# Hybrid decoder trunk on one core: places of the mixing steps in the other stage's program from two tables, in place of even spacing

## The reference, cut to what matters

```python
h = rms_norm(x, norm_mix_g[i]);  z = h @ w_cols
zs = token_shift(z[..., :RWKV_COLS], mu_shift[i])       # r, k, v and three low-rank inputs
...
y = rwkv7_scan(rh, decay, kh, vh, kk, a)                # 8 heads x 64, a state passed from token to token
swa_out = swa_sink_attention(zq, zk, zvv, sinks[i], rel_bias)   # window 128, 8 query heads, 2 kv heads
x = x + concatenate([rwkv_out, swa_out]) @ w_out[i]
u = rms_norm(x, norm_mlp_g[i])
x = x + square(relu(u @ w_ff_up[i])) @ w_ff_down[i]
e = rms_norm(p[i] @ ple_proj[i], ple_norm_g[i])
x = x + e * sigmoid(x @ ple_gate[i])
return rms_norm(x, final_norm_g)
```

## The kernel before

| step | TensorE | waits for |
|---|---|---|
| 0, 1 | keys and scores; decay and rate (L703) | step 1: `small` by ScalarE |
| 2, 3 | norms; transposed probabilities (L672) | step 3: probabilities (L1397) by VectorE's step 2, which waits for ScalarE's step 1 and goes on with the scan (L1423) and a scaling (L1427) |
| 4, 5, 6 | norms spread; output gate; bonus (L735) | `knorm`, `kk`, `rk` by VectorE |
| 7 to 9 | second half of the attention, transposes | probabilities again (L1397) |
| 10, 11 | scores of the recurrence (L766); `av` | `kappa_t`; masked scores |
| 12 to 16 | five doubling steps of the inverse (L787) | VectorE: add, mask, transpose (L1494) |
| 17 to 23 | the inverse put together; state (L828), both chunks | the step before, by VectorE |
| 24 | `y` | nothing new; behind it GpSimd squares `y` (L543) |
| 27 | `y` transposed (L876) | the normed `y` (L1544); behind it VectorE makes `rw` (L1549) and GpSimd adds and multiplies (L546, L549) |
| 28 | nothing | SyncE stores `rw` (L426) |

## Time and profile before

### The profile page before, as it was taken

How to read it: one execution, slowest core, us unless ns; L and a number is a source line. 1 busy time by engine, 2 the same in 40 slices (tenths; PEclk the granted TensorE clock), 3 DMA queues, 4 the chain that set the end, 5 groups by cost and what they waited for, 6 DMA issues and landing times.

```text
span 3061.8 us, 54864 instructions
## 1 busy us (share of the span) xinstructions
PE 2866.5 (94%) x23922; PEld 2282.5 (75%) x23922; DVE 1350.0 (44%) x2329; ACT 1187.6 (39%) x1939; POOL 1146.6 (37%) x540
## 2 busy tenths in 40 slices
PE   7988989999999989989999999998999899999997
PEld 6767767777777767767777777776777678788876
DVE  4265474535444344563535353644453535311114
ACT  4354344244434242453443333534242425422224
POOL 3433333342334333433333333324344334344442
PEclk9999999999999999999999999999999999999999
DMA  6532433353232313342223233332232224333332
GB/s 201 182 115 89 132 109 94 109 182 91 63 97 73 99 59 99 121 147 66 86 80 92 66 99 101 128 101 77 81 97 78 61 88 149 117 97 96 97 97 76
DMA packets 335948, 313.31 MB, mean 102 GB/s; under 512 B 13499, under 2 KB 288220, under 8 KB 335708
## 3 DMA queue, kind: packets, MB, share of 16 engines
q1 hardware_dynamic: 331312, 305.38, 32.5%
q10 hardware_dynamic: 4396, 4.41, 0.5%
HBM read 271.98 MB, written 39.32 MB: 102 GB/s over the span
## 4 chain that ended last, share of the span: by engine, by line
PE 64%; DVE 8%; ACT 5%; POOL 3%; issue 3%; ACTq 0%; POOLq 0%; DVEq 0%
PE ps L895 11%; PE ps L899 10%; PE ps L898 10%; PE ps L943 7%; PE ps L947 6%; PE ps L946 6%; POOL w_lo L505 2%; PE ps L641 1%; PE ps L787 1%; PE ps L644 1%; ACT bm L1108 1%; PE ps L645 1%; ACT work L1130 1%; PE ps L663 1%; PE ps L680 1%
## 5 line engine op out<-in xcount | busy, mean ns | idle before, releaser
L505 POOL TENSOR_TENSOR w_lo<-wraw_f,w_hi 128x1024 fp32r<-128x1024 f32 x408 | 990.9, 2429 | 1600.2 <-ACT w_hi L1025 1600.0
L1025 ACT ACTIVATE w_hi<-wraw_f 128x1024 fp32r<-128x1024 f32 x408 | 430.3, 1055 | 643.6 <-PE ps L895 550.2
L895 PE MATMUL ps<-w_hi,h_hi 128*128 128x512 f32 x1280 | 525.0, 410 | 26.2 <-POOL w_lo L505 19.7
L899 PE MATMUL ps<-w_hi,h_lo 128*128 128x512 f32 x1280 | 503.3, 393 | 0.0
L898 PE MATMUL ps<-w_lo,h_hi 128*128 128x512 f32 x1280 | 502.7, 393 | 0.0
L943 PE MATMUL ps<-act_hi,w_hi 128*128 128x512 f32 x1024 | 423.9, 414 | 27.0 <-DVE x L1604 19.6
L946 PE MATMUL ps<-act_lo,w_hi 128*128 128x512 f32 x1024 | 405.8, 396 | 0.0
L947 PE MATMUL ps<-act_hi,w_lo 128*128 128x512 f32 x1024 | 405.2, 396 | 0.0
L895 PEld LDWEIGHTS ps<-w_hi,h_hi 128*128 128x128 f32 x1280 | 242.4, 189 | 94.1 <-POOL w_lo L505 27.6
L1214 ACT ACTIVATE h_hi<-tmp 128x512 fp32r<-128x512 f32 x128 | 80.9, 632 | 545.9 <-DVE tmp L1586 545.9
L899 PEld LDWEIGHTS ps<-w_hi,h_lo 128*128 128x128 f32 x1280 | 242.3, 189 | 53.0
(11 more groups left out here) (223 smaller groups left out, 4428.6 us busy)
## 6 DMA issues: line engine op xcount, KB each, us to landing
wraw_f<-in_w_ff_up SPq DMA_DIRECT2D x256, 256.0 KB, 3.4
wraw_f<-in_w_ff_down SPq DMA_DIRECT2D x128, 512.0 KB, 3.8
wraw_f<-in_w_in SPq DMA_DIRECT2D x80, 512.0 KB, 4.4
zT<-tmp SPq DMA_DIRECT2D x80, 256.0 KB, 2.1
wraw_f<-in_w_out SPq DMA_DIRECT2D x32, 512.0 KB, 5.0
wraw_f<-in_w_gate SPq DMA_DIRECT2D x32, 512.0 KB, 3.9
zs<-zT SPq DMA_DIRECT2D x16, 896.0 KB, 7.4
h_lo<-mixT SPq DMA_DIRECT2D x4, 2048.0 KB, 9.8
```

Of the source, the lines that this page charges most:

```text
L505: G.tensor_tensor(w_lo[:, n % 2, :], raw[:, n % 4, :], w_hi[:, n % 2, :].bitcast(F32), ALU.subtract).then_inc(w_lo_done, 1)
L895: mm = T.matmul(ps[:, j, :], ah, wh, start=(first and k == 0), stop=False)
L899: mm = T.matmul(ps[:, j, :], al, wh, start=False, stop=(final and k == 1))
L1025: S.activation(w_hi[:, n % 2, :], raw[:, n % 4, :], ACT.Copy).then_inc(w_hi_done, 1)
```

## The change

`side_by_side` takes a tuple of 116 places instead of a number of quanta and a head. Before, step i stood at `head + (quanta - head) * i // 116`: from 4 to 113 beside the projection, from 2 to 148 beside a finish (gaps of 1 and 2 in a fixed rhythm). Now the places are read from two tables. All engines still run the same instructions; only the order in which steps and quanta follow each other in each engine's program differs, the same on all five.

```diff
-LEAD = 150
-def side_by_side(fill, tiles, quanta, head):
-    given, steps = 0, MIX_STEPS * len(tiles)
-    for i in range(steps):
-        want = head + (quanta - head) * i // steps
-        while given < want:
+BESIDE_PROJ = (3, 4, 4, 5, 7, 8, 10, 13, 14, 14, 14, 15, 17, 19, 21, 22, 24, 25, 26, 27, 27, 27, 27, 28, 28, 29, 29, 31, 31, 32, 34,
...
+BESIDE_FIN = (0, 1, 3, 4, 5, 5, 7, 7, 8, 9, 10, 13, 13, 14, 15, 19, 21, 23, 24, 26, 27, 29, 30, 31, 31, 33, 33, 35, 36, 36, 37, 39,
...
+def side_by_side(fill, tiles, places):
+    assert len(places) == MIX_STEPS * len(tiles)
+    given = 0
+    for i, place in enumerate(places):
+        while given < place:
             next(fill)
             given += 1
         next(tiles[i // MIX_STEPS])
...
-    side_by_side(one_after_another(proj(1), proj(2), proj(3)), [mix(t) for t in range(TPB)], 3 * 2 * ZT - 6, 4)
+    side_by_side(one_after_another(proj(1), proj(2), proj(3)), [mix(t) for t in range(TPB)], BESIDE_PROJ)
     for b in range(1, BLOCKS):
-        side_by_side(fin(b - 1), [mix(t) for t in range(b * TPB, (b + 1) * TPB)], LEAD, 2)
+        side_by_side(fin(b - 1), [mix(t) for t in range(b * TPB, (b + 1) * TPB)], BESIDE_FIN)
```

## The result

The changed kernel takes 2918.09 us (median of four runs, 2913.71 to 2920.3) against 3063.01 for the kernel before, measured beside it on the same chips (3059.04 to 3066.16). The ratio is 0.9526, with a 95% interval of 0.9508 to 0.9543 (the later intervals are of the same kind): 145 us faster. The forecast was 76 us, with a range that ended 12 us above what was measured. The direction was right, the size was half.

The account below looks back on a forecast made before the run. TensorE, busy 2866.5 of 3061.8 us, was taken as the bound. Three finish blocks at 28 us (21 waits, 5 clock, 2 turns) plus 18 in the projection made 102; a quarter off, 76, gave 2984 us, range 2930 to 3035.

Parts of the forecast that it names:

- rival 1: The forecast itself: a good part of TensorE's waits goes, 2930 to 3035 us; chance 0.79.
- Part (b): Steps with GpSimd work at a chunk's start delay the next chunk's `w_lo`: 1.2 to 3.1 us each; mid-chunk, no wait.
- The clock: Stretches at 1.2 GHz follow waits of over about 2 us; 5 us a finish block recoverable, 4 in the projection.
- Rival 3: Slower: 27 steps at gap 0 wait for their predecessor, up to 6.9 us each, 3110 us; chance 0.07.
- Rival 4: More goes, the clock recovering altogether and tiles not disturbing each other: below 2930 us; chance 0.04.
- the projection stage: Stage ahead of the finish blocks: 10 us of idle time, 4 of clock and 4 of turns saved, 18 us.
- the turns: TensorE turning to a step and back, 0.2 us estimated; fewer turns save 2 us a finish block, 4 in the projection.
- A quarter off gives 76 us: Discount on the 102 us sum for two conflicts in a row or a queue not seen.
- The residual waits, 17 us a block: TensorE idle time left in a finish block, against 38 us before: 21 us saved.
- Step 12 at gap 0: First doubling step of tiles 0, 1 and 3 beside a finish, no quantum ahead: 1.6 us each.
- Step 24 at 66: Tile 1's step ahead of which GpSimd squares `y`, at a chunk's start beside a finish: about 1.2 us lost.
- Steps 27 and 28 at 156: Tile 3 beside a finish: `rw` queued behind VectorE's transpose work, the second gate chunk behind `rw`, 3.5 us.

Follow-up runs that it names:

- e4: Even spacing (the kernel before) with steps 24, 27 and 28 beside each finish moved one quantum, off chunk starts: 3033.13 us (0.9904).
- e10: Changed kernel with a gap of 1 instead of 0 ahead of step 12 of tiles 0, 1 and 3 beside each finish: 2920.21 us (0.9529).
- e12: Changed kernel with step 27 of tile 3 at place 154 instead of 156 beside each finish: 2917.49 us (0.9522).
- e13: Changed kernel with only step 1 of each tile beside each finish one quantum later, at chunk starts (2, 38, 72, 112): 2943.14 us (0.9605).
- e14: Even spacing with the moves of e4, steps 0 to 3 and neighbours moved, step 1 in the middle of its chunk in all tiles: 2986.48 us (0.9745).
- e11: Even spacing with the moves of e4 and some twenty more, step 1 at a chunk's start in tiles 0, 2 and 3: 3016.25 us (0.9847).
- e8: Changed kernel with a smoothed table: projection places remade with fewer gaps of 0, some finish steps of tiles 0, 1 and 3 moved: 2938.58 us (0.9598).
- e9: Changed kernel with steps 27, 28 of tiles 1 and 2 at chunk starts, the next tile's steps 0 and 1 one quantum behind: 2945.69 us (0.9615).
- e5: Changed kernel with every place of the finish table one quantum higher, all gaps the same: 3050.85 us (0.996).
- e1: New finish table alone, old even spacing beside the projection: 2936.72 us (0.9589).
- e6: Changed kernel with every place of the finish table two quanta higher, all gaps the same: 2983.18 us (0.9739).

## Why the prediction was wrong

**Held.** What bounds the kernel, the repetition of three equal blocks and the untouched last one. The mechanism of rival 1: waits go, TensorE's work is the same. Part (b) for steps 24 and 27: its prices make 7.6 us a block, 23 in three, with the clock behind them on top, and e4 measured 30. Three entries of the residual list: step 5 at gap 0 (predicted 0.9, measured 0.95 from start to start), step 1 of tile 1 at 37 (2.0 and 1.8), the transposes ahead of the gate (2.3 and 2.2 from start to start). The clock: 5 us a block predicted, 6.2 measured (31 distances between fill matmuls of 0.43 us in place of 0.23 became none: 31 x 0.20). Rival 3, slower by gaps of 0, did not come: no wait at such a gap in the finish block is above 1 us, and in the projection stage they reach 2.1. Rival 4, below 2930, had 0.04 and is what happened.

**Right by luck: the projection stage.** 18 us were predicted and 18.2 measured, but of other parts. Idle time fell by 14.7 us where I had 10, the clock gave about 2.4 (12 fewer distances at half rate) where I had 4, and about 1 is left for the turns, where I had 4. Single terms were further off: the waits for the probabilities, of which I had 3.2 us of new ones in tile 0, fell from 6.0 to 0.8; the bonus fell to 0, not to 2; step 1 of tile 2, whose 3.1 us were to go with one quantum, still waits 2.26. The number itself is loose: nine traces with this projection table reach the first finish block between 643.0 and 649.7 us, six with even places between 661.9 and 669.7.

**Failed: the sum per finish block**, in two terms. The gap of 70 us between 76 and 145.6 is 26 from the first, and 43 from the second with the smaller terms beside it.

1. *"A quarter off gives 76 us."* I took a discount for conflicts that I had not seen. No such loss showed in the total: the sum of 102 was already low, not high. 26 us.
2. *The residual waits, 17 us a block.* Measured: 7.2 of idle time. Step 12 at gap 0, three times 1.6, cost 0 (e10; its operand hangs on step 10, not 11). Step 24 at 66, 1.2, cost 0. Steps 27 and 28 at 156, 3.5, cost 0.8, and moving step 27 to 154 doesn't get it (e12). The bonus, step 11, "a step behind adds" and the weight chunk, 2.2, cost 0. Together nearly 11 us of the 17 were not there, and about 1 us stood where I had none (the transposes at quanta 17 to 20). So 31 us of idle time went, where I had 21. About 4 us more a block are an estimate: there are 20 waits fewer, and each makes the matmul behind it some 0.2 us later than its idle time says (the one at 1451.13 waits 3.08 us and starts 3.47 behind the one before it, in place of 0.23). With 6.2 of clock that leaves about 3 for the turns in the block, whose length fell by 44.3; I had 28. The three blocks gave 127.5 for 84.

Two of the signs were wrong too: TensorE's busy time was to stay within 10 us and fell by 42, and the idle time ahead of the doubling steps was to stay or rise and fell from 6.6 to 0 us in the finish block, from 9.0 to 5.6 in the projection stage.

**Not seen: step 1's side of the chunk.** Part (b) of the prediction looked at GpSimd, since the profile names GpSimd's `w_lo` as the releaser. Part of these waits come from ScalarE, one engine further up: in the block of before, GpSimd had been idle for more than 10 us ahead of the `w_lo` behind two of the six such waits (1.6 and 1.1 us of 10). Step 1's 5.6 us of ScalarE ahead of `w_hi` cost 25 to 30 us in all when three or four of four such steps in a block lie at a chunk's start (e13, and e14 against e11, where a few neighbours moved too). In e13 some 3 us a block of this are the probabilities, since step 3 stands a quantum nearer. I priced step 1 by its own wait alone. It did not falsify the sum, since the new table has all four in the middle (1, 37, 71, 111), but it is behind the miss of e11, part of those of e8 and e9, and 13 us a block of that of e5.

**The gain, taken apart.** From even spacing: steps 24, 27 and 28 off the chunk starts, 30 us (e4); steps 0 to 3 and their neighbours moved as well, with step 1 in the middle, 78 in all (e14); the whole finish table, which also spreads the doubling steps (6.4 us a block in e14, 0 after) and keeps `x` adds clear, 126 (e1); both tables, 145. That the order of the edits would give the same shares isn't shown. The price of a side isn't one number either: the four steps 1 bring 5.4 us of `w_lo` a block in e13, and 13.0 in e5, where steps 2 and 3 lie a quantum later as well. The rest of the 133 us of the shift isn't taken apart by step.

## What to carry to other kernels

When a step is inserted into in-order programs of several engines beside a double-buffered stream, ask on which side of the stream's producer it lands on *each* engine; a shift of one quantum moved this kernel by 133 us with every gap unchanged. The releaser that the profile names is the last of a chain: look whether it was itself idle (8.88 us here), and go one engine up. A gap of 0 costs only if what the step needs is not made yet (0 us beside the finish, 2.01 in the projection stage, for the same step), so read the dependence before pricing it, and don't take a discount off a sum without a wait to name for it.

## What the hardware showed

- *The clock falls late and behind the wait.* In e11 the wait of 3.16 us ends at 1308.79; the next matmuls still start 0.23 us apart, from 1310.05 on 0.40 to 0.43, at a granted clock of 0.50 (1.2 GHz) over 1310.4 to 1313.0. In the kernel after, the longest wait between 656 and 2790 us is 1.8 us, and no fill matmul there runs at 1.2 GHz. In the whole run there were 24 such stretches before and 7 after, all ahead of 656 us or at the end; some 145 distances between fill matmuls were at half rate before, 45 after. So a long wait can cost more than its own length. The length of one wait doesn't decide it. In e6 a single wait of 1.54 us is followed by a granted clock of 0.50; in e13 two waits of 0.82 and 1.11 us, 2.2 us apart, are too (1262.5 to 1265.5); and in e4 a wait of 3.17 us, ended at 1958.85, is not. Busy time and granted clock (the value before the last two) behind the wait in e6, and then in e4:

```profile
1551.00:1554.00 3.00, 3.00 (x8) 2.31 (x7) 2.36 (x7) 2.97 (x4) 2.15 (x2) 0.50 0.20 60
```

```profile
1958.80:1962.00 3.20, 3.15 (x12) 2.32 (x13) 3.09 (x7) 0.00 (x0) 0.00 (x0) 1.00 0.00 0
```

- *A table load costs its own 1.28 us.* The sigmoids end at 1301.38, the load begins at 1301.39 and the first exponential at 1302.69. The Trainium skill (ScalarE: Activation LUTs, section "What ACT_TABLE_LOAD costs") adds a drain and comes to about 2.66 us a switch; this trace shows no such time, nor do the others: around the loads of the kernel before and of the kernel after, the median distance to the instruction ahead is 0.02 us and to the one behind 0.01. There were 106 loads before and 102 after, so the feared growth did not come.
